# Smaller tiles in a DeltaNet inversion, regrouped state updates and an earlier copy, in a four-layer trunk kernel on one core

## What is computed

```python
a = jnp.where(strict, jnp.einsum("nbhid,nbhjd->nbhij", kb, k) * decay, 0.0)
lower = a + jnp.eye(C, dtype=a.dtype)
sol = lax.linalg.triangular_solve(lower, rhs, left_side=True, lower=True, unit_diagonal=True)
u, w = sol[..., :dv], sol[..., dv:]
def step(state, xs):
    v_new = u_c - jnp.einsum("bhcd,bhde->bhce", w_c, state)
    o_c = (jnp.einsum("bhcd,bhde->bhce", q_c * jnp.exp(g_c)[..., None], state)
           + jnp.einsum("bhij,bhje->bhie", qk_c, v_new))
    state = (state * jnp.exp(g_last)[..., None]
             + jnp.einsum("bhcd,bhce->bhde", k_c * jnp.exp(g_last - g_c)[..., None], v_new))
```

## Time and profile before

| | |
|---|---|
| Three runs | 2406.86, 2405.82, 2406.66 us (median 2406.66) |
| The profiled execution | 2407.66 us, its span 2405.9 us |
| TensorE | busy 2198.0 us, 91% of the span |
| VectorE, ScalarE, POOL | busy 1353.7, 1120.1, 195.8 us |
| Mean granted TensorE clock | 0.962 of full speed |
| Chain that ended last | 75% TensorE, 14% VectorE, 5% issue, 5% ScalarE |
| L933, the products of the inversion | 4608 + 1152 records, 160.6 + 43.9 us |
| L796, `head_proj` | 1024 records, 400.2 us |

### The profile page before, as it was taken

The page is one execution under the profiler, slowest core; times in us unless marked ns, Lnnn a source line. Parts: engine busy times, 40 slices in busy tenths (PEclk is TensorE's granted clock), DMA queues, the critical chain, the costliest instruction groups (busy, mean ns, idle before and its releaser), DMA issues.

```text
span 2405.9 us, 39650 instructions
## 1 busy us (share of the span) xinstructions
PE 2198.0 (91%) x16240; PEld 1508.3 (63%) x16241; DVE 1353.7 (56%) x2550; ACT 1120.1 (47%) x1927; POOL 195.8 (8%) x281
## 2 busy tenths in 40 slices
PE   6999999988998999899899998998999999887996
PEld 3666666655776565577655655775666666655874
DVE  2555555524898232489821215897455555526896
ACT  3344444413765243376523315765444444405774
POOL 0311111101000100100010001000211111100000
PEclk8999999988999899899999998999999999988998
DMA  8232333223886434388633343985211111112880
GB/s 348 89 111 111 127 129 127 114 90 124 295 301 247 161 142 175 124 282 304 244 130 139 140 158 129 312 306 221 73 54 43 41 60 41 41 55 88 305 312 40
DMA packets 56747, 380.94 MB, mean 158 GB/s; under 512 B 6384, under 2 KB 10480, under 8 KB 12000
## 3 DMA queue, kind: packets, MB, share of 16 engines
q1 hardware_dynamic: 51552, 373.05, 43.1%
q10 hardware_dynamic: 4608, 4.20, 0.5%
q0 software_dynamic: 384, 0.89, 0.1%
HBM read 374.01 MB, written 4.10 MB: 157 GB/s over the span
## 4 chain that ended last, share of the span: by engine, by line
PE 75%; DVE 14%; issue 5%; ACT 5%; DMA 1%; SPq 0%; POOL 0%; ACTq 0%; DVEq 0%; POOLq 0%
PE ps L796 14%; PE ps L742 7%; PE ps L933 7%; PE ps L1406 5%; DVE e_wlo L2678 5%; PE ps L1410 5%; PE ps L1409 5%; PE ps L713 3%; PE ps L1189 3%; PE ps L1362 2%; DVE bufx L2696 2%; PE ps L758 2%; PE ps L1292 2%; DVE scratch L2246 2%; ACT e_whi L1595 1%
## 5 line engine op out<-in xcount | busy, mean ns | idle before, releaser
L2678 DVE TENSOR_TENSOR e_wlo<-ring,e_whi 128x1024 fp32r<-128x1024 f32 x384 | 456.2, 1221 | 88.8 <-ACT e_whi L1595 72.8
L1595 ACT ACTIVATE e_whi<-ring 128x1024 fp32r<-128x1024 f32 x384 | 402.7, 1060 | 117.2 <-PE ps L1410 114.3
L796 PE MATMUL ps<-bufh,ring 128*128 128x384 f32 x1024 | 400.2, 510 | 23.9 <-ACT scratch L1595 21.0
L1595 ACT ACTIVATE scratch<-ps 128x384 f32<-128x384 f32 (+3 forms) x343 | 142.8, 437 | 305.9 <-PE ps L933 178.7
L796 PEld LDWEIGHTS ps<-bufh,ring 128*128 128x128 f32 x1024 | 172.9, 190 | 117.1 <-issue 47.0
L1406 PE MATMUL ps<-e_whi,e_hs 128*128 128x512 f32 x512 | 210.7, 412 | 28.0 <-DVE e_wlo L2678 24.7
L1410 PE MATMUL ps<-e_whi,e_hs 128*128 128x512 f32 x512 | 200.6, 392 | 0.0
L1409 PE MATMUL ps<-e_wlo,e_hs 128*128 128x512 f32 x512 | 199.9, 390 | 0.0
L1595 ACT ACTIVATE scratch<-ps,scratch 64x128 f32<-64x128 f32 x192 | 69.5, 362 | 240.4 <-PE ps L1045 237.2
L742 PE MATMUL ps<-bufo,ring 128*128 128x384 f32 x512 | 170.4, 496 | 9.8 <-DVE bufo L2314 8.6
L933 PEld LDWEIGHTS ps<-scratch 64*64 64x64 f32 x4608 | 144.7, 135 | 36.0 <-issue 25.0
(11 more groups left out here) (304 smaller groups left out, 3512.5 us busy)
## 6 DMA issues: line engine op xcount, KB each, us to landing
ring<-in_moe SPq DMA_DIRECT2D x192, 1024.0 KB, 4.9
ring<-in_w_ada SPq DMA_DIRECT2D x96, 1024.0 KB, 5.2
ring<-in_gdn_w_in SPq DMA_DIRECT2D x32, 1024.0 KB, 6.4
ring<-in_gdn_w_out SPq DMA_DIRECT2D x8, 1024.0 KB, 5.2
ring<-in_gqa_w_in SPq DMA_DIRECT2D x6, 1024.0 KB, 4.8
ring<-in_gqa_w_out SPq DMA_DIRECT2D x4, 1024.0 KB, 5.1
ring<-in_mla_w_out SPq DMA_DIRECT2D x4, 1024.0 KB, 7.6
ring<-in_mla_w_in SPq DMA_DIRECT2D x3, 1024.0 KB, 4.9
```

The costliest lines, as they stand in the source:

```text
L796: last = mm(ps[:, head_bank(n, m), 0:T], w[:, m % 2, kt, :], bufh[:, kt, :], start=(kt == 0), stop=(kt == KT - 1))
L1595: return op(out, in_, ACT.Copy, **kw)
L2678: return tt_(e_wlo[:, b, :], w, e_whi[:, b, :].bitcast(F32), ALU.subtract)
```

## The change

**Inversion on 32x32 tiles.** Only the 32x32 diagonal blocks are worked on in jobs 1 to 12. A product is 24 matmuls of 32x32 by 32x32, one on each of the four groups of 32 partitions in turn; its tiles, copies and additions are 128x192. Job 0 has 24 such transposes and 12 more for the off-diagonal blocks, which go to bank 2 and are copied by VectorE to `g_cross`. Jobs 13 and 14 (`cross_product`) are 12 matmuls each. ScalarE writes the diagonal blocks of `g_final` in four copies, VectorE the off-diagonal ones in four; POOL clears `g_final` once a layer, and makes the first operand in three operations for one.

**Scan.** `os` is split into `st` (the two state updates) and `os` (the output): `st(0) st(1) os(0) os(1)`, the same for rounds 2 and 3. `ks(4)` multiplies all 128 tokens of a tile for each direction. **v's copy**, `head_raw(l, n, 2)`, stands ahead of `values(4)`, and the state's DMA after `values(5)`. **Gram** waits on `qk_ready` alone, but for head 0.

```diff
             def product(hh, job):
                 a, b, bank = INVERSE[job]
                 for d in range(2):
                     for t in range(TT):
-                        for half in range(2):
-                            rows = slice(64 * half, 64 * half + 64)
-                            at = 64 * (TT * d + t)
-                            last = mm(ps[rows, bank, at:at + 64], g_inv[a][rows, d, t, :],
-                                      C("cid")[rows, :] if b is None else g_inv[b][rows, d, t, :],
+                        at = 32 * (TT * d + t)
+                        for g in range(4):
+                            left = g_n[quarter(g), d, t, 32 * (g % 2):32 * (g % 2) + 32] if job == 0 else \
+                                g_inv[a][quarter(g), d, t, :]
+                            right = C("cid")[quarter(g), :] if b is None else g_inv[b][quarter(g), d, t, :]
+                            last = mm(ps[quarter(g), bank, at:at + 32], left, right, start=True, stop=True)
+                if job == 0:
+                    for t in range(TT):
+                        for g in range(4):
+                            d = upper(g)
+                            last = mm(ps[quarter(g ^ 1), INVERSE[2][2], 32 * t:32 * t + 32],
+                                      g_n[quarter(g), d, t, 32 - 32 * (g % 2):64 - 32 * (g % 2)], C("cid")[quarter(g), :],
                                       start=True, stop=True)
+                last.then_inc(inv_mm, 1)
+
+            def cross_product(hh, job):
+                bank = INVERSE[job][2]
+                for t in range(TT):
+                    for g in range(4):
+                        if job == 13:
+                            out, left, right = quarter(g ^ 1), g_cross[quarter(g), t, :], g_inv["x"][quarter(g), 1 - upper(g), t, :]
+                        else:
+                            out, left, right = quarter(g), g_inv["pb"][quarter(g), upper(g), t, :], g_crossed[quarter(g), t, :]
+                        last = mm(ps[out, bank, 32 * t:32 * t + 32], left, right, start=True, stop=True)
                 last.then_inc(inv_mm, 1)
...
             def gram(l, n):
-                pe.wait_ge(nrm_dev, nn + 1)
                 pe.wait_ge(qk_ready, nn + 1)
-                pe.wait_ge(silu_done, nn * 3 + 2)
                 if n == 0:
+                    pe.wait_ge(silu_done, nn * 3 + 2)
...
                         s = SCAN[r, d]
-                        at = P * s.t + 64 * s.half
-                        mm(ps[chunk_rows(s), s.bank, 0:P], qkv[:, 1, at:at + CHUNK], g_state[:, s.seg, d, :],
+                        rows, at, n = (slice(0, P), P * s.t, P) if r == 4 else (chunk_rows(s), P * s.t + 64 * s.half, CHUNK)
+                        mm(ps[rows, s.bank, 0:P], qkv[:, 1, at:at + n], g_state[:, s.seg, d, :],
...
                 pe.wait_ge(w_done, hh + 1)
+                st(0)
+                st(1)
                 os(0)
                 os(1)
...
ScalarE, scan:
+                if more:
+                    head_raw(l, n, 2)
                 values(4)
+                values(5)
                 act.wait_ge(s_done, hh * 10 + 8)
                 act.dma_start(O["state"][hh], g_state[:, 1, :, :]).then_inc(st_out, 16)
-                if more:
-                    head_raw(l, n, 2)
-                values(5)
...
VectorE, end of invert:
-                tt_(flat(g_final), flat(g_inv["x"]), ps[:, INVERSE[14][2], 0:T], ALU.add).then_inc(inv_x, 1)
+                for g in range(4):
+                    last = V.tensor_copy(g_final[quarter(g), upper(g), :, 32 - 32 * (g % 2):64 - 32 * (g % 2)],
+                                         ps[quarter(g), INVERSE[14][2], 0:32 * TT].rearrange("p (t c) -> p t c", c=32))
+                last.then_inc(inv_x, 1)
```

More of the change, by code:

```diff
@@ L451, in trunk @@
         g_decay4 = g_decay.rearrange("p (d t c) -> p d t c", d=2, t=TT)
-        g_inv = {name: c(2, TT, 64) for name in ("n", "nd", "ndt", "t32", "t64", "pa", "pb", "x")}
+        g_n = c(2, TT, 64)
+        g_inv = {name: c(2, TT, 32) for name in ("nd", "ndt", "t32", "pa", "pb", "x")}
+        g_cross, g_crossed = c(TT, 32), c(TT, 32)
         g_final = c(2, TT, 64)
@@ L610, in gqa_tile_done, with quarter, upper @@
                 used(eng, mix_unit(1, "w", pos // 2))
+        def quarter(g):
+            return slice(32 * g, 32 * g + 32)
+        def upper(g):
+            return g % 2
         def chunk_rows(step):
@@ L1057, in os @@
                                start=True, stop=True).then_inc(st_mm, 1)
+                def os(r):
+                    new = g_v2[:, SCAN[r, 0].seg, SCAN[r, 0].half, :]
                     first, second = sorted((SCAN[r, 0], SCAN[r, 1]), key=lambda s: s.c0)
@@ L1796, in invert @@
                 taken(hh, 12)
-                taken(hh, 13)
+                cross_taken(hh)
+                final_diagonal(hh)
                 if more:
@@ L2329, in invert @@
                 dve.wait_ge(inv_mm, hh * 15 + 1)
-                src = ps[:, INVERSE[0][2], 0:T].rearrange("p (m c) -> p m c", c=64)
-                for dst, mask in (("ndt", "c16"), ("t32", "c32"), ("t64", "c64")):
-                    last = tt_(g_inv[dst].rearrange("p d t c -> p (d t) c"), src, spread(C(mask), 2 * TT), ALU.mult)
-                    if dst == "ndt":
-                        last.then_inc(inv_x, 1)
-                last.then_inc(inv_x, 1)
+                bank = INVERSE[0][2]
+                src = ps[:, bank, 0:T // 2].rearrange("p (m c) -> p m c", c=32)
+                tt_(g_inv["ndt"].rearrange("p d t c -> p (d t) c"), src, spread(C("c16"), 2 * TT), ALU.mult).then_inc(inv_x, 1)
+                V.tensor_copy(g_cross.rearrange("p t c -> p (t c)"), ps[:, INVERSE[2][2], 0:32 * TT]).then_inc(inv_x, 1)
+                tt_(g_inv["t32"].rearrange("p d t c -> p (d t) c"), src, spread(C("c32"), 2 * TT), ALU.mult).then_inc(inv_x, 1)
                 if more:
                     mask_rows(l, n, 0)
-                added(hh, 3, 2)
+                added(hh, 3, 3)
                 if h and l == 0:
@@ L2347, in invert @@
                     mask_rows(l, n, 1)
-                added(hh, 8, 4)
+                added(hh, 8, 5)
                 if h:
```

87 lines of the change are left out of this document (55 added, 32 removed).

## The result

The changed kernel takes **2375.6 us** (median of 4 runs, 2368.9 to 2378.6), the kernel before 2406.6 us beside it: ratio 0.987, interval 0.985 to 0.988. It is faster by 31 us. The forecast was 98 us faster, 2309 us; 2375.6 lies in the range of 2290 to 2390. So the direction was right and two thirds of the gain are missing. The profiled execution took 2373.4 us, 34.3 us less than the profiled one of before.

The account below looks back on a forecast made before the run. TensorE was taken to bound the DeltaNet heads. From 2407.7 us, minus 80 (inversion), 20.3 (v's copy) and 2 (last heads), plus 0.6, 1 and 2.8, came 2309.8, forecast as 2309 us; range 2290 to 2390.

Parts of the forecast that it names:

- v's copy: Scan: moved ahead of `values(4)`, it lets z's `head_proj` start 1.45 us earlier, 14 times, 20.3 us saved.
- Gram: Start of `gram`: dropping two finished waits gains nothing, since it hangs on the state update; 7 us is the upper end.
- The views of before: Profile before: TensorE busy 384.6 of 400.0 us in layer 0's window and 353.3 of 373.8 in layer 3's.
- The state updates: Scan: `st(1)` must wait for `values`, a loss of 0.1 us twice a head with filling, 2.8 us.
- `v_tokens`: Layer 3: it waits on VectorE's convolution, so job 0's 0.13 us earlier end is lost 8 times, 1 us.
- The end of the inversion: VectorE's four copies for one addition take 0.36 us more, mostly hidden before `vn(0)`; 0.6 us may show.
- The size of a round: Inversion: four 32x32 tiles at once take 31.6 ns, against 58.3 ns a pair before; 80 us saved for 16 heads.
- a round has a floor: Rival, chance 0.15: 32 columns cost as much as 64, so 6 us saved replace 80; 2383 us.
- Does the filling still cover the waits?: Inversion: 0.6 us to spare between products, so no new wait with filling; unfilled last heads save 2 us.
- TensorE takes in records no faster than now: Rival, chance 0.12: inversion's 696 records a head for 360, at 29.2 ns each, cost +157 us; 2545 us.
- both signs: Signs of a wrong forecast: granted clock in the DeltaNet layers under 1.00, or TensorE waiting inside an inversion with filling.

## Why the prediction was wrong

**The views of before** were read rightly: TensorE set the pace of the heads, and what was taken from it came back where nothing else ran short, in layer 3.

**v's copy**: forecast 20.3 us, measured 20.4 alone. Right, and it is two thirds of what the change gained, a gain that has nothing to do with the tiles. **Gram**: forecast nothing, and its waits went from 7.2 to 6.1 us. **The state updates**: forecast a loss of 2.8 us by a new wait for `values`. In the trace after,

```profile
207.85 0.65 PE L1075 MATMUL ps<-scratch 64*64 64x128 f32 x8
...
209.28 1.10 PE L1086 MATMUL ps<-scratch 64*128 64x128 f32 x8
210.31 0.71 PE L1094 MATMUL ps<-scratch 128*128 128x128 f32 x4
210.86 0.81 PE L808 MATMUL ps<-bufh,ring 128*128 128x384 f32 x2
```

from `vn` to `head_proj` it takes 3.01 us, as in rows 9 (1852.17 - 1849.16). I took the merged row of four `values` to end when the last one is done, but the wait did not come; the measured loss of 6 us is not in the heads, so it doesn't bear the term out. **`v_tokens`**: forecast a loss of 1 us; its wait went from 4.7 to 4.0 us. **The end of the inversion**: no wait appears at `vn`; right.

**The size of a round**: 31.6 ns were forecast, 37 ns measured. The slope between 384 and 64 columns, drawn on to 32, came out 5.4 ns too low. 174 x 5.4 ns x 16 = 15 us of the missing 64. The rival *a round has a floor* falls: a further product adds 0.445 us and not 0.70. The Trainium skill's page TensorEngine Tiling, section Instruction Overhead, advises against cutting a small dimension further since a matmul has a floor of about 60 columns; the rows here contradict it for four tiles at once, 37 ns against 58.3.

**The step that failed** is "Does the filling still cover the waits?", with the answer "So there is no new wait in the inversions with filling". It asked only for waits between engines. Whether the instructions themselves arrive in time was never asked, though the rival *TensorE takes in records no faster than now* had the right count, 696 records a head for 360. That rival was half right. In a burst a record takes 9.3 ns (it turned to slower at 16.7 ns), so within a product the records are no limit. Over several products 26 to 32 ns a record is the limit, and it came near the rival's 29.2 ns only by luck: that was the slope of the 64x64 products (0.70 us for 24 records; the 72 records in 2.31 us are one per 32.1 ns), whose pace the array set. Between the products the long records of `head_proj` give the fetch time to catch up. In layer 3 that suffices nearly: 1.6 us of listed pauses in seven heads. In layer 0 the pauses make 17 us, and 7 of them go when the loads are cut. In the last heads there are no long records between: 10 us, and the clock. The Trainium skill's page TensorE: Matmul & The Clock Gate, section Back-to-back issue gap, says that start to start stays at about 25 ns or above. Rows of 48 to 144 records here, at 9.3 ns, disagree for different tiles; the long run at 26 to 32 ns is of its size, but what set it here was the supply of blocks.

The pauses make 29 of the missing 64 us (27.1 + 1.2 + 1.0) and the round's size 15. The other 20 us I put down to the fallen clock and to pauses too short for the list of waits; this is argued, not measured by itself, but the stages bear it out. Layer 3's seven heads kept a clock of 1.00, and there pauses and rounds (1.6 and 6.6 us) leave nothing of the missing 7.6. What is left over lies where the clock fell: 7 us in layer 0's seven heads, 13 us in the two last heads. In the stretch of 384 us of layer 0 a clock of 0.96 means 8% of it at half speed, 31 us, and half of that, 15 us, is the most it can have cost. I had named both signs beforehand: the clock in the layers under 1.00, and TensorE waiting inside an inversion that has filling.

## What to carry to other kernels

When a change multiplies instructions, count them as a resource of their own: instructions per stretch by the rate at which they can be brought (here an estimated 26 to 32 ns for a record with its weight load, over a stretch of several packets), beside the array time. A saving in array time counts only down to that rate, and less where large loads start at the same moment. A wait without a releaser in the middle of a group of equal instructions, in a list that had none, is how it looks in a profile, and an instruction packet that ends shortly before the group goes on (here 1.2 to 1.6 us) confirms it; where the place of work is free, put long instructions between the short ones and large loads elsewhere.

## What was not expected of the hardware

Four 32x32 float32 tiles on the four groups of rows and columns ran at once, 9.3 ns a record, with results in one PSUM bank. Instruction blocks of 16.4 KB come over the same DMA engines as the data: with these at 0.98 busy from 460 to 464 us no block came, and the pause of 4.00 us that began at 463.08 ended only 1.49 us after the next block had. And where such pauses stand the granted clock falls more than before: in layer 3 two pauses of 1.53 and 1.68 us in an unfilled head stand ahead of 41 us at 0.50, with a third of 0.98 us within them, whereas the same head before kept 0.88. It does not follow every pause: in layer 0 the clock fell to 0.50 in five of the seven full heads, and stayed at 1.00 in two that have pauses of 2.02 us and of 1.14 and 1.02 us. Why filling held it up only in part is open. A hybrid, with 64x64 tiles in layer 0's inversions or in the last heads and 32x32 tiles elsewhere, was not tried.
